# A hybrid decoder trunk on one core: norm weights' row by DMA, mixed halves made in the output stage, weights split early, and x ahead of the constants

## Time and profile before

| | us |
|---|---|
| median of three runs | 3322.2 (3314.61 to 3323.11) |
| profiled execution, its own time | 3327.27 |
| its span, first to last instruction | 3325.5 |
| TensorE busy in it | 3218.9 |
| VectorE busy | 2018.1 |
| ScalarE busy | 1243.4 |
| GpSimd busy | 1902.7 |

### The profile page before, as it was taken

The page is one execution under the profiler, slowest core; times in us unless marked ns, Lnnn a source line. Parts: engine busy times, 40 slices in busy tenths (PEclk is TensorE's granted clock), DMA queues, the critical chain, the costliest instruction groups (busy, mean ns, idle before and its releaser), DMA issues. The chain is left out here.

```text
span 3325.5 us, 47826 instructions
## 1 busy us (share of the span) xinstructions
PE 3218.9 (97%) x15066; PEld 2605.4 (78%) x15066; DVE 2018.1 (61%) x4092; ACT 1243.4 (37%) x1869; POOL 1902.7 (57%) x1317
## 2 busy tenths in 40 slices
PE   8889999999999999999899989999999999999999
PEld 6568888888887788888665668888888887787887
DVE  4556676752224888888536647575742224888888
ACT  3543333334443333333425633333332223333333
POOL 0005888888888555554000005888888886655554
PEclk9999999999999999999899999999999999999999
DMA  5915565566667999998409105565566668999998
GB/s 188 333 51 134 119 150 119 135 148 143 142 149 239 346 353 346 357 349 302 128 28 310 46 31 136 119 149 117 134 146 145 143 147 258 350 352 344 348 353 304
DMA packets 398808, 680.92 MB, mean 205 GB/s; under 512 B 145153, under 2 KB 239361, under 8 KB 398465
## 3 DMA queue, kind: packets, MB, share of 16 engines
q1 hardware_dynamic: 218368, 519.89, 46.3%
q0 software_dynamic: 155648, 134.82, 19.8%
q10 hardware_dynamic: 24704, 25.17, 2.3%
HBM read 559.79 MB, written 119.93 MB: 204 GB/s over the span
## 5 line engine op out<-in xcount | busy, mean ns | idle before, releaser
L1744 POOL DMA_INDIRECT gate_matrix<-pe_misc x768 | 1287.3, 1676 | 428.5 <-issue 233.6
L2013 PE MATMUL psum<-split,ex_ah 128*128 128x512 f32 x2976 | 921.4, 391 | 14.5 <-DVE ex_al L2458 14.3
L408 PE MATMUL psum<-up_hhi,up_hi 128*128 128x512 f32 x2048 | 798.1, 390 | 0.0
L408 PE MATMUL psum<-up_hlo,up_hi 128*128 128x512 f32 x2048 | 796.8, 389 | 0.0
L408 PE MATMUL psum<-up_hhi,up_lo 128*128 128x512 f32 x2048 | 796.8, 389 | 0.0
L399 DVE TENSOR_TENSOR up_lo<-up_raw,up_hi 128x1024 fp32r<-128x1024 f32 x256 | 314.0, 1227 | 759.2 <-ACT up_hi L395 690.2
L2013 PEld LDWEIGHTS psum<-split,ex_ah 128*128 128x128 f32 x2976 | 555.2, 188 | 144.4 <-DVE ex_al L2458 27.7
L2013 PE MATMUL psum<-split,ex_al 128*128 128x512 f32 x1488 | 579.1, 389 | 0.0
L1754 POOL DMA_INDIRECT ex_gv<-in_v,ga_at x256 | 274.6, 1073 | 339.2 <-DVE x_sb L2408 320.8
L408 PEld LDWEIGHTS psum<-up_hhi,up_lo 128*128 128x128 f32 x2048 | 384.4, 188 | 79.9
L408 PEld LDWEIGHTS psum<-up_hhi,up_hi 128*128 128x128 f32 x2048 | 384.5, 188 | 79.4
(11 more groups left out here) (369 smaller groups left out, 3337.3 us busy)
## 6 DMA issues: line engine op xcount, KB each, us to landing
up_raw<-in_uT SPq DMA_DIRECT2D x256, 512.0 KB
ro_wq<-in_v SPq DMA_DIRECT2D x256, 512.0 KB
gelu<-up_z SPq DMA_DIRECT2D x256, 256.0 KB
pe_misc<-gelu SPq DMA_DIRECT2D x256, 192.0 KB
ex_gm<-gate_matrix SPq DMA_DIRECT2D x124, 384.0 KB
gate_matrix<-ga_at ACTq DMA_DIRECT2D x8, 3072.0 KB, 12.4
gate_matrix<-ga_at SPq DMA_DIRECT2D x8, 3072.0 KB, 23.4
ro_wq<-in_peer_wq SPq DMA_DIRECT2D x32, 512.0 KB
```

Source lines behind the costliest of these rows:

```text
L408: last = pe.matmul(self.ps[:, a, :], w[:, a, dc, :], h[:, dc, :], start=(dc == 0 and m == 0), stop=(dc == DC - 1 and m == 2))
L1744: pool.indirect_dma_start(place, bass.IndirectOffsetOnAxis(ap=to[:, j:j + 1], axis=0), gates[:, j:j + 1], None, compute_op=ALU.add).then_i ...
L2013: last = pe.matmul(psy[:, o, :], w[:, par, a, toks], v[:, par, a, cols], start=False, stop=(final and m == 2))
```

## The change

1. `front0`, start. SP issues x0, x1, then the parameters, then x2, x3. ScalarE begins with a square root of a zero (so that its table is loaded), and does square and root tile by tile; VectorE likewise mean square and scale. |lambda|, its exponential, the softplus and a scaled gain come later: ScalarE's behind the root of the memory norm, VectorE's behind the split of chunk 3.
2. `front0`, DMAs. Behind the loads of chunks 8 and 9 SP issues one DMA each that copies the norm_ffn weights of a layer from their columns in the parameters to a row in device memory; the stage ends only when they have landed.
3. `front0`, end. Five gelus go ahead of the last copy of transposed shares; ScalarE and VectorE split chunk 0 of the output weights; GpSimd multiplies the first three chunks of scan and gelu, VectorE the other three. The splitting of the mixed channels moves to `out_norm`.
4. `out_norm`. The diagonal, the products with ones and the eviction are gone; SP loads `row` from device memory, spread over the partitions, behind the weight loads. In layer 0 (`ready` = 1, `mix` = the eight mixed chunks) the halves of the mixed chunks are made here, in the order 0, 6, 7, 1, then the split of weight chunk 1, then 2 to 5. The banks are taken in the order 0, 1, 4, 5, 6, 7, 2, 3. In layer 1 `ready` is 2 and nothing is mixed.
5. `attention`. At the beginning of steps 31 and 35 ScalarE and VectorE split chunks 0 and 1 of w_out1.

```diff
 # attention (SPLIT = (N // 2, N // 2 + 4), N = 62)
 dve: for step in range(N + 5):
+         if step in SPLIT:
+             n = SPLIT.index(step)
+             dve.wait_ge(split.sem, split.done(n))
+             dve.tensor_tensor(wlo[:, n, :], w_out[:, n, :], whi[:, n, :].bitcast(F32), ALU.subtract)
 act: for step in range(N + 4):
+         if step in SPLIT:
+             n = SPLIT.index(step)
+             act.wait_ge(loaded.sem, loaded.base + 16)
+             act.activation(whi[:, n, :], w_out[:, n, :], ACT.Copy).then_inc(split.sem, 1)
 # front0, sync
-            sp.dma_start(k.params[:], k.dram["params"]).then_inc(s["params"].sem, 16)
             for t in range(TT):
                 sp.dma_start(x[:, t, :], k.dram["x"][t * P:(t + 1) * P, :]).then_inc(s[f"x{t}"].sem, 16)
+                if t == 1:
+                    sp.dma_start(k.params[:], k.dram["params"]).then_inc(s["params"].sem, 16)
...
+                if n in (8, 9):
+                    at, w = OFF[f"norm_ffn{n - 8}"]
+                    sp.dma_start(rows[n - 8, :].rearrange("(c p) -> c p", p=P), k.dram["params"][:, at:at + w].rearrange("p c -> c p"),
+                                 allow_slow_non_contiguous=True).then_inc(s["rows"].sem, 16)
...
+            sp.wait_ge(s["rows"].sem, s["rows"].base + 16 * LAYERS)
 # front0, gpsimd
+            pool.wait_ge(s["scanned"].sem, s["scanned"].done(0))
+            for i in range(NL // 2):
+                pool.wait_ge(s["gelu"].sem, s["gelu"].done(i))
+                pool.tensor_tensor(tnh[:, i, :], tnh[:, i, :], y[:, i, :], ALU.mult)
 # front0, scalar
-            act.wait_ge(s["params"].sem, s["params"].base + 16)
-            act.activation(sp_[:, 0, :], lam, ACT.Abs)
-            act.drain()
-            act.activation(sp_[:, 1, :], sp_[:, 0, :], ACT.Exp, scale=-1.0).then_inc(s["yexp"].sem, 1)
+            act.wait_ge(s["zero"].sem, s["zero"].done(0))
+            act.activation(small[:, 60:61], ga.zeros()[:, 0:1], ACT.Sqrt)
+            (then square(t), root(t) for t = 0 to 3, high(0), high(1), wait for the parameters)
...
             act.activation(mstd, mssq, ACT.Sqrt).then_inc(s["mroot"].sem, 1)
+            (Abs, drain and Exp of lambda, as above)
...
             keep_turned(6)
-            keep_turned(7)
             act.drain()
-            for i in range(NL):
-                if i == NL - 1:
-                    step(13)
-                    act.drain()
-                act.activation(y[:, i, :], y[:, i, :], ACT.Gelu_apprx_tanh).then_inc(s["gelu"].sem, 1)
-            (highs of the eight mixed chunks)
+            for i in range(NL - 1):
+                gelu(i)
+            keep_turned(7)
+            act.wait_ge(s["wo"].sem, s["wo"].base + 16)
+            act.wait_ge(s["prod"].sem, s["prod"].done(12))
+            act.activation(whi[:, 0, :], wo[:, 0, :], ACT.Copy).then_inc(s["split"].sem, 1)
+            step(13)
+            act.drain()
+            gelu(NL - 1)
 # front0, vector (softplus_of and qgain moved behind low(3))
-            for i in range(NL):
+            for i in range(NL // 2, NL):
+                if i == NL - 1:
+                    dve.wait_ge(s["split"].sem, s["split"].done(0))
+                    dve.tensor_tensor(wlo[:, 0, :], wo[:, 0, :], whi[:, 0, :].bitcast(F32), ALU.subtract)
                 dve.wait_ge(s["gelu"].sem, s["gelu"].done(i))
                 dve.tensor_tensor(tnh[:, i, :], tnh[:, i, :], y[:, i, :], ALU.mult)
-            (lows of the eight mixed chunks)
 # out_norm; first = (0, 6, 7, 1, 2, 3, 4, 5)
+            sp.dma_start(row, bc(rows[l:l + 1, :], [P, D])).then_inc(s["row"].sem, 16)
 pe:
-            (products of ones and the diagonal, wait for their eviction)
             for dc in range(DC - 2):
-                pe.wait_ge(s["wlo"].sem, s["wlo"].done(dc))
-                for o in range(2 * TT):
+                if dc >= ready:
+                    pe.wait_ge(s["wlo"].sem, s["wlo"].done(dc - ready))
+                if mix:
+                    pe.wait_ge(s["mixlo"].sem, s["mixlo"].done(first.index(dc)))
+                for o in (0, 1, 4, 5, 6, 7, 2, 3):
+                    if mix and dc == 0 and o == 2:
+                        pe.wait_ge(s["mixlo"].sem, s["mixlo"].done(first.index(DC - 1)))
                     last = products(dc, o, False)
 act:
-            high(0)
-            high(1)
-            (eviction of the row)
+            for dc in first if mix else ():
+                act.activation(up.hhi[:, dc, :], mix[dc], ACT.Copy).then_inc(s["mixhi"].sem, 1)
+                if dc == 1:
+                    high(1)
 dve:
-            (the diagonal)
-            for dc in range(DC):
+            for n, dc in enumerate(first if mix else ()):
+                dve.wait_ge(s["mixhi"].sem, s["mixhi"].done(n))
+                dve.tensor_tensor(up.hlo[:, dc, :], mix[dc], up.hhi[:, dc, :].bitcast(F32), ALU.subtract).then_inc(s["mixlo"].sem, 1)
+                if dc == 1:
+                    low(1)
+            for dc in range(2, DC):
                 low(dc)
```

More of the change, by code:

```diff
@@ L335, in attention @@
     loaded.passed(16)
+    split.passed(2)
     zeroed.passed(16 * NZERO)
@@ L473, in softplus_of, with front0 @@
     dve.drain()
-def front0(k, x, up, wq, misc, ga, rope, wo, kv, last, gmat):
+def front0(k, x, up, wq, misc, ga, rope, wo, kv, last, gmat, rows):
     nc = k.nc
@@ L498, in front0 @@
         "ksq": 2, "kmean": 1, "keps": 1, "kroot": 1, "kr": 1, "kb": 1, "kn": 1,
-        "exps": 2, "left": 2, "rooted": 2, "gelu": NL, "mixed": NL, "mixhi": DC,
+        "exps": 2, "left": 2, "rooted": 2, "gelu": NL, "scanned": 1, "split": 1, "rows": 16 * LAYERS,
         "scored": A, "maxed": A, "expd": A, "scaled": A, "turn": 2 * A, "stored": 2 * A, "summed": A})
@@ L822, in _ @@
             high(1)
+            act.wait_ge(s["params"].sem, s["params"].base + 16)
             for dc in range(DC):
@@ L963, in shares @@
                 last.then_inc(s["scaled"].sem, 1)
[L965 to L975, removed]
+            for t in range(TT):
+                mean_square(t)
+                scale(t)
             low(0)
             low(1)
+            dve.wait_ge(s["params"].sem, s["params"].base + 16)
             for dc in range(DC):
@@ L1521, in first_queries, with out_norm @@
     return last
-def out_norm(k, l, x, up, peer_, wo, wo2, scratch):
+def out_norm(k, l, x, up, peer_, wo, wo2, scratch, rows, ready, mix):
     nc = k.nc
     held = wo.shape[1]
-    s = Stage(k, {**{f"w{i}": 16 for i in range(DC - held)}, "whi": DC, "wlo": DC, "prod": DC - 2 + TT, "added": TT,
-                        "ones": 1, "diag": 1, "row": 1, "kept": 1,
+    s = Stage(k, {**{f"w{i}": 16 for i in range(DC - held)}, "whi": DC - ready, "wlo": DC - ready, "prod": DC - 2 + TT, "added": TT,
+                        "row": 16, "mixhi": DC if mix else 0, "mixlo": DC if mix else 0,
                         "sq": TT, "ms": TT, "root": TT, "xn": TT, "turned": TT, "hi": TT, "lo": TT})
@@ L1580, in turn @@
                 last.then_inc(s["turned"].sem, 1)
[L1582 to L1586, removed]
-            for dc in range(DC - 2):
-                pe.wait_ge(s["wlo"].sem, s["wlo"].done(dc))
-                for o in range(2 * TT):
-                    if dc == 0 and o == 2 * TT - 2:
-                        pe.wait_ge(s["kept"].sem, s["kept"].done(0))
+            for dc in range(DC - 2):
+                if dc >= ready:
[5 more added lines that the diff above has]
+                        pe.wait_ge(s["mixlo"].sem, s["mixlo"].done(first.index(DC - 1)))
                     last = products(dc, o, False)
                 last.then_inc(s["prod"].sem, 1)
-            pe.wait_ge(s["wlo"].sem, s["wlo"].done(DC - 1))
+            pe.wait_ge(s["wlo"].sem, s["wlo"].done(DC - 1 - ready))
             for t in range(TT):
@@ L1691, in _ @@
             add(1)
+            dve.wait_ge(s["row"].sem, s["row"].base + 16)
             scale(0)
```

66 lines of the change are left out of this document (30 added, 36 removed).

## The result

| | before | after |
|---|---|---|
| median of six runs, us | 3317.2 (3312.9 to 3323.1) | 3346.0 (3339.8 to 3347.5) |
| profiled execution, its span | 3325.5 | 3345.7 |

The ratio of the runs is 1.0078, 95% interval 1.0067 to 1.0090 (the ratio of the two medians is 1.0087): slower, by 28.9 us between the medians, where I had forecast 9.6 less and given slower a chance of 0.07. The two profiled spans differ by only 20.2: that of before is one of the kernel's long ones, and 5 us of its excess lie in the second PEER stage (1336.4 us against 1331.2).

A forecast was written before the change was run, and what follows sets the result against it. Longest links in the chain of waits were PEER products (20%) and v loads (8%), both untouched; shifts elsewhere should come through whole. Terms -2.3 - 8.3 - 3.6 + 4.6 = -9.6 gave 3312.6 on the median, forecast 3313 us, range 3304 to 3321.

The forecast's parts named there:

- part 6: Row DMAs of norm weights in the first mixer: 2.7 us each over sixteen engines, hidden by up to 4 us; 0.
- Rival C: Row DMAs run on one DMA engine, holding back chunk 10's weights: 48 us later, 3360 us; chance 0.05.
- 1 start: Start of the kernel: first product near 16.7 instead of 19.38 us, part lost again; 2.3 us saved, bounds 1.1 and 2.9.
- 2, 3 hand-over of layer 0: First mixer's end to its output product: out stage starts 5.9 us earlier; 8.3 saved in all, bounds 7.4 and 9.1.
- 5 splits in the attention: Layer 1's attention, steps 31 and 35: the splits delay TensorE; 4.6 us lost, bounds 0 and 5.5.
- 4 head of layer 1: Layer 1's out stage: both chunks already split, 4.45 us saved less 0.85 for the clock; 3.6 saved.
- rival B: End of first mixer: POOL's multiplies, contending with VectorE, end it and add 4.8 us; 3317.4 us; chance 0.12.
- Rival A: Layer 1's attention: the two splits are absorbed at no cost; -14.2 us, 3308 us; chance 0.18.

The follow-up runs named there:

- r10: Kernel after with only layer 0's row DMA, behind chunk 8; layer 1's row comes as an input: 3329.0 us.
- r1: Kernel after with both rows of norm weights as an input laid out in a row, so without the two row DMAs: 3321.0 us.
- r2: Kernel before with only the two row DMAs and the stage's wait for them added; nothing reads the rows: 3350.4 us.
- r3: Kernel after with the two row DMAs moved to the start, behind the gate weights and ahead of chunk 2: 3333.3 us.
- r7: r1 with all six multiplies of scan and gelu on VectorE, none on GpSimd: 3314.0 us.
- r6: r1 with one late split (chunk 0, step 63) instead of two in mid-attention; chunk 1 split in the output stage: 3309.1 us.
- r8: r6 with r7's multiplies: rows as an input, one late split, all multiplies on VectorE: 3308.7 us.
- r11: Kernel after with both row DMAs behind the mixer's last load of weights: 3327.5 us.
- r9: Kernel before with the new start alone (x0 and x1 first, square root table first, softplus later): 3317.9 us.
- r4: Kernel after with the eight zeroing DMAs issued by GpSimd instead of ScalarE, row DMAs unmoved: 3338.4 us.

## Why the prediction was wrong

The step that failed is part 6, "I take nothing". I priced 1024 pieces of 4 bytes by the time that DMA engines spend on such pieces, divided it by sixteen, and set the 2.7 us against the 4 us that a chunk's load had to spare. One DMA costs 12.5 us of the mixer (r10), both 27.0 (r1), and in the kernel before 29.4 (r2). The row of 43 ns was a scatter that GpSimd issues, in a queue of its own; no row of before had such pieces behind an issue of SP. Two things were missing. The pieces cost the issues and the transfers around them far more than engine time (r3); by what mechanism stays open. And the room I reckoned with was not there: the windows before show a DMA share of 0.96 to 1.05 in that stretch, because ScalarE zeroes the gate matrix, whose DMAs have a queue of their own but run on the same DMA engines. The 5.5 us a DMA that I worked out from eight engines fell short too; how many engines moved the pieces no run shows. The row of the DMA share was to be had; I had looked at the queue that loads the weights. Rival C had the sign and the place, but rested on one engine holding the pieces, and on 48 us.

Step by step, by the two profiled executions (-9.6 forecast, +20.2 measured):

| step | forecast | measured |
|---|---|---|
| 1 start | -2.3 | -3.7: product at 15.6 rather than 16.7; nothing lost again at the turned memory (VectorE's writes 3.5 earlier); a round of square and root took 1.48, not 1.85 |
| 6 rows | 0 | +26.9 (r1: 26.0 to the last eviction, 27.0 to S) |
| 2, 3 hand-over of layer 0 | -8.3 | -5.9 |
| end of that stage | 0 | +1.6 |
| 5 splits in the attention | +4.6 | +8.2 |
| 4 head of layer 1 | -3.6 | -3.1 |
| the rest, PEER stages above all | 0 | -3.8 |

- Hand-over of layer 0: the sequence is right. In r7, with the clock at 1.00, the stage starts 2.3 us after the last eviction (forecast 2.35) and the split of chunk 2 follows 7.2 later (7.4). In the kernel after 1.1 went to GpSimd and 2.3 to the clock, for which I had 0.8: it was 0.50 from 204.8 to past 209, after a stop of 4.3. A stop of 3.2 was followed by 0.50 in r1 and r6 and by 1.00 in r7 and r8, so its length alone does not decide.
- GpSimd takes 1.9 us a multiply where I had 1.6, and slows VectorE while it does: three scans 4.49 instead of 3.45. That is rival B's contention, at 1.1 us where GpSimd starts early enough (r7); the rule of the Trainium skill cited with it agrees with the trace.
- End of that stage: after the wait for the last low half (2.47 us in both kernels) the clock fell to 0.50 near 244 us and was back before 248; before it stayed at 1.00. From the split of chunk 2 to the last eviction it is 53.8 us in every kernel with the new output stage but r11, and 52.2 in before, r2, r9 and r11. So something in the new stage makes this fall likely; I did not find what.
- Attention: both stalls are where and as long as forecast (2.1 and 2.6 against 2.1 and 2.5). Missing was what I had counted at the hand-overs: after each of the two stops TensorE went on at the lower clock, 3.5 us for both. Rival A is refuted.
- Head of layer 1: mechanism as forecast, size 0.5 short.

The differences in S and in A, added, come within 5 us of the difference in the medians for all kernels but r4 (7). The rest lies in the PEER stages, whose length moves by several us from run to run; I did not settle whether part of it belongs to an edit.

## What to carry to other kernels

Price a DMA by what waits behind it, at its own issue and at every other engine whose DMAs run on the same DMA engines, and look at the DMA share of that stretch first; a transfer of a few KB in pieces of 4 bytes is worth an input laid out otherwise. Work put into an idle share has its place where the engines already wait: the same split cost 4 us in the middle of a pipeline and nothing in its last steps. Whatever makes TensorE stop may cost twice, for the stop and for the products at the lower clock behind it; the second part came after some stops and not after others of the same length (1.6 us at either hand-over), so it belongs into the range of a forecast.

## What the runs showed of the hardware

- A DMA of 1024 pieces of 4 bytes, 4 KB in all, delayed the output stage by 12.5 us (r10), as long as a zeroing DMA of 3 MB took to land before (12.4).
- With these pieces under way, zeroing DMAs took 14 and 25 us to issue from ScalarE (after), 18 (r10) and 31 (r2), a load 6 to 13 us from SP; GpSimd's own issues stayed at 1.4 to 1.6 us (r4). SP issued a load in 0.33 us while ScalarE stood at its 25.
- GpSimd multiplying 128x512 tiles (1.7 to 1.9 us each) stretched VectorE's two-input instructions: multiply 0.62 to 1.6 us, scan 1.15 to 1.5, subtraction of 128x1024 1.22 to 2.30.
- The same stop of TensorE was followed by either clock: 3.2 us by 0.50 (r1, r6) and by 1.00 (r7, r8); 1.69 us by 0.50 (after, r8) and by 1.00 (r6).
